# Twenty-seven matrix products whose results nobody reads, taken out of a two-block transformer kernel

## The chip, the cores and the metric

One core of a Trainium2 chip runs the whole kernel. The metric is the device time of one execution in microseconds, lower is better. All arithmetic is in 32-bit floating point.

## What is computed

One sequence of 256 tokens with 1024 features goes through two models, one behind the other.

```python
def reference(x, c, ctx, ...):
    x = first_block(x, c, ctx, ...)
    return second_block(x, c_2, ...)

# first_block, layer 0: short convolution mixer and SwiGLU, on x and on the context
mod = jax.nn.silu(c) @ w_ada[i] + b_ada[i]
mod_c = jax.nn.silu(c_ctx) @ w_ada[i] + b_ada[i]
h = _modulate(_rms_norm(x, norm_mix[i]), sh1, sc1)
hc = _modulate(_rms_norm(ctx, norm_mix[i]), sh1c, sc1c)
# layer 1: neighbourhood attention (x against x and the context) and SwiGLU, on x

# second_block: a norm and one wide projection, sparse attention and an RWKV-7
# recurrence side by side, gated and merged; then a mixture of experts
p_group = jax.nn.softmax((xt @ wg_router).astype(f32), axis=-1)
g_sel = jnp.argmax(p_group, axis=-1)                       # one of 4 groups
top_v, top_i = lax.top_k(e_in, TOP_K_EXPERTS)              # 2 of its 8 experts
acc + cw[:, None] * ((jax.nn.silu(xt @ wg) * (xt @ wu)) @ wd)   # over 32 experts
```

The weights of the 32 experts are 201 MB of the 419 MB that the kernel reads.

## The kernel before, in words

The program is written engine by engine: each engine has its own list of instructions in a fixed order, and semaphores order the lists among each other. No scheduler and no pool moves anything. Activations lie feature-major in SBUF (128 features by 256 tokens for each of 8 slices). SyncE (`block.sync`, line 507) streams all weights into rings of slots in one order, each load behind a wait for the products that last used the slot. GpSimd loads the modulation weights of later layers and adds up halves of weights, VectorE and ScalarE make the norms, the activations and the attention's softmax, and TensorE does the products.

The stages that matter here:

- **Start.** `ada_first(s)` (line 1239) multiplies the two condition vectors by block `s` of four blocks (2 MB each) of modulation weights; each call waits for its block with `slot_landed`. Between the calls stand the first norm's sums (`norm_sums`, line 1259) and the spread of its reciprocal roots over the partitions (`norm_spread`, line 1268). Behind the fourth block ScalarE copies the four rows out (line 856), `ada_columns` turns them into columns (line 1249), VectorE makes shift and scale of them (lines 2329 and 2315), and ScalarE (line 867) and VectorE (line 2730) apply these to the normed activations, slice by slice. The first products of the convolution (lines 1319 and 1327) take the slices as they come.
- **Attention of the second block.** `dsa_attention` on TensorE goes over pairs of heads: scores, a piece of a gate's projection (line 1575) as filling, transposes (line 1598), products with the values.
- **Last norm and router.** `norm(5)` is `norm_sums`, a wait for ScalarE and VectorE, and `norm_spread`. Then come the router's logits (line 2242), their transposes (line 2249), and transposes of the activations (line 2252). VectorE finds the group and the two experts in a chain of 20 small instructions (lines 3119 to 3134). The rank products (lines 2260 to 2264) give each token its place at its experts, VectorE turns them into places and into the count of the busiest expert, and each engine loads this count into a register and branches on it (`count_of`, line 495).
- **Experts.** `pe_gathered` gathers the tokens of four experts with one-hot products (line 1676), goes through gate and up weights (line 1726) and down weights (line 1708), eight times four experts. SyncE has loaded the first four slots of gate and up weights ahead; the load that follows (line 567) waits for the first of TensorE's products to free its buffer, and all further loads follow on it in the same manner.

`keep_on(bank, n)` issues `n` products of the identity with 256 columns of the constants into a PSUM bank that nobody reads. It waits for nothing and signals nothing:

```python
def keep_on(bank, n):

    for i in range(n):
        pe.matmul(PS[:, bank, 0:256], ident, C[:, 0:256], start=True, stop=True)
```

One 32-bit product is two MATMUL instructions and two LDWEIGHTS in the trace.

Of the kernel before, what the change touches and what calls it, by code (L numbers as in the profile page):

```python
# [156 lines left out]
def build(nc, xin, ada, cond, vecs, consts, colmask, dist, reset, rpb, rank_c, W, out):  # L157
    plan = plan_stream()
    MMB = count_products()
    with ExitStack() as ctx:  # L160
# [13 lines left out]
        C = sb("C", NCONST)  # L174
# [10 lines left out]
        PS = ctx.enter_context(nc.psum_tensor("PS", [P, 8, 512], F32))  # L185
# [9 lines left out]
        ident, ones, bo64 = con("ident"), con("ones"), con("bo64")  # L195
# [41 lines left out]
        NORMS = [(0, 0, 2, 0), (24, 0, 2, 0), (0, 1, 2, 0), (24, 1, 1, 0), (0, 2, 1, 1), (24, 2, 1, 1)]  # L237
# [987 lines left out]
        def _(pe):  # L1225
            pe.wait_ge(sem("cond"), 1)
            pe.wait_ge(sem("consts_in"), 16)

            def keep_on(bank, n):

                for i in range(n):
                    pe.matmul(PS[:, bank, 0:256], ident, C[:, 0:256], start=True, stop=True)

            def ada_first(s):

                slot_landed(pe, "ada0", s)
# [34 lines left out]

            def norm(n):
                norm_sums(n)
                keep_on(4, NORMS[n][2] + 1)
                norm_spread(n)
                keep_on(4, 2)

            def norm_ahead(n, left):

# [300 lines left out]
            def dsa_attention():  # L1580
# [33 lines left out]
                for p in range(pairs):  # L1614
                    if p + 1 < pairs:
                        scores(p + 1)
                    gate_part(0, 7, GATE_CUTS[p], GATE_CUTS[p + 1])
                    turn(2 * p)
                    if p == 0:
                        keep_on(5, 3)  # L1620
                    turn(2 * p + 1)
                    if p >= 1:
                        pv(p - 1)
# [233 lines left out]
            norm_sums(0)  # L1857
            ada_first(1)
            norm_spread(0)
            keep_on(4, 4)  # L1860
            ada_first(2)
            keep_on(4, 4)
            ada_first(3)
            ada_columns()
            keep_on(4, 2)
            conv_in_folded()
            conv_out_folded()
            ffn_in_folded()
# [120 lines left out]
            for i in range(12):  # L1989
# [12 lines left out]
                if i == 6:  # L2002
                    for k in range(KD):
                        g = 32 * (k % 4)
                        mm = pe.matmul(PS[g:g + 32, 7, 0:SEQ], vec("w_i", k * 8, k * 8 + 32), XN[:, k * SEQ:(k + 1) * SEQ],
                                       start=(k < 4), stop=(k >= 4))
                    mm.then_inc(sem("wi_mm"), 1)
                if i == 8:
                    pe.wait_ge(sem("wi_done"), 1)
                    for t in range(2):  # L2010
                        mm = pe.matmul(PS[:, 7, 256 + t * 8:264 + t * 8], WIT[:, t * P:(t + 1) * P], con("eight"),
                                       start=True, stop=True)
# [146 lines left out]
            for c in range(NCH):  # L2159
# [3 lines left out]
                for hp in range(HP):  # L2163
                    for h in range(2):
                        dst = PS[64 * h:64 * h + 64, 0, hp * 64:hp * 64 + 64]
                        if c:
                            pe.matmul(dst, f64(KK, c, hp, h), st[64 * h:64 * h + 64, hp * 64:hp * 64 + 64],
                                      start=True, stop=False)
# [21 lines left out]
                for hp in range(HP):  # L2190
                    for h in range(2):
                        dst = PS[64 * h:64 * h + 64, 2, hp * 64:hp * 64 + 64]
                        pe.matmul(dst, c64(BT, c, hp, h), SA[64 * h:64 * h + 64, hp * 64:hp * 64 + 64],
                                  start=True, stop=False)
                        mm = pe.matmul(dst, c64(KT, c, hp, h), c64(VT, c, hp, h), start=False, stop=True)
                mm.then_inc(sem("state_mm"), 1)
                for hp in range(HP):
                    for h in range(2):
                        o = (hp % 2) * 256 + c * CH
                        dst = PS[64 * h:64 * h + 64, 3 + hp // 2, o:o + CH]  # L2200
                        if c:
                            pe.matmul(dst, st[64 * h:64 * h + 64, hp * 64:hp * 64 + 64], f64(RR, c, hp, h),
                                      start=True, stop=False)
# [50 lines left out]
                                      ident)  # L2254
                mm.then_inc(sem("xt_mm"), 1)

            keep_on(4, 7)
            pe.wait_ge(sem("indicated"), 1)
            pe.wait_ge(sem("rank_in"), 16)
            pe.matmul(PS[:, 6, 0:NE], UPPER, IND[:, 0, :], start=True, stop=True)  # L2260
# [1 line left out]
            pe.matmul(PS[:, 6, NE:2 * NE], UPPER, IND[:, 1, :], start=False, stop=True)  # L2262
            pe.matmul(PS[:, 6, 2 * NE:3 * NE], ones, IND[:, 0, :], start=True, stop=False)
            pe.matmul(PS[:, 6, 2 * NE:3 * NE], ones, IND[:, 1, :], start=False, stop=True).then_inc(sem("ranked"), 1)
            keep_on(4, 3)
            busiest = count_of(pe)
            with pe.If(busiest < CAP + 1):
                pe_gathered()
# [1053 lines left out]
```

## Time and profile before

| | us |
|---|---|
| median of 3 runs | 1849.72 |
| lowest and highest | 1849.64, 1849.98 |
| profiled execution, whole | 1848.07 |
| its span, first to last instruction | 1845.9 |
| busy in it: TensorE | 1647.6 |
| VectorE | 920.6 |
| ScalarE | 278.6 |
| GpSimd | 521.1 |

The profile is of one execution. The difference of 2.2 us between its time and its span lies around the program. "PE" is TensorE's products, "PEld" its weight loads, which run beside them; "DVE" is VectorE, "ACT" ScalarE, "POOL" GpSimd, "SP" SyncE. An instruction is named by its line, and what it writes and reads by `out<-in`. "Idle before" is the pause of the engine ahead of an instruction, with the instruction or transfer that ended it; the ends of products are modelled. The granted clock is the share of TensorE's 2.4 GHz that the chip let through: 1.00 is 2.4 GHz and 0.50 is 1.2 GHz. It is recorded where it changes, so that the view shows 1.00 ahead of the first record.

### The profile page before, as it was taken

The page shows a single profiled execution, that of the slowest core. Times are in us where ns is not written, and L with a number is a line of the kernel's source. Part 1 is how long each engine was busy: PE and PEld are TensorE (multiplying, and loading weights), DVE is VectorE, ACT ScalarE, POOL GpSimd, SP SyncE. Part 2 cuts the span into 40 slices and gives each one's busy share as a digit, 9 for nine tenths or more (in the row PEclk, how much of TensorE's full clock was granted, in tenths as well). Part 3 has the DMA queues.
Part 4 walks back from the last instruction along what each step waited for, and adds up shares of the span by engine and source line. Part 5 has one row for each costly group of instructions (what it writes and reads, how often), then busy time and mean ns, then how long its engine had stood idle before and what let it go on. Part 6 is the DMA issues. An engine that isn't in the chain of part 4 may idle for free.

```text
span 1845.9 us, 26016 instructions
## 1 busy us (share of the span) xinstructions
PE 1647.6 (89%) x11170; PEld 1284.0 (70%) x11170; DVE 920.6 (50%) x1439; ACT 278.6 (15%) x612; POOL 521.1 (28%) x375
## 2 busy tenths in 40 slices
PE   6999999999999999999999999999999745574547
PEld 3888778888888868768999887778786312221223
DVE  3999678888672465683876534565223000000001
ACT  3000130000000221272001022341202000000000
POOL 2554455667632249001773212300000000000000
PEclk9999999999999999999999999999999887887779
DMA  9552134557441440025665980520097999999998
GB/s 398 190 228 103 69 142 170 171 180 274 167 156 63 160 183 1 15 85 226 224 228 225 365 327 1 200 81 26 2 399 306 424 430 432 428 432 429 434 431 339
DMA packets 44047, 422.02 MB, mean 229 GB/s; under 512 B 4912, under 2 KB 5312, under 8 KB 22944
## 3 DMA queue, kind: packets, MB, share of 16 engines
q1 hardware_dynamic: 24336, 345.26, 45.9%
q0 software_dynamic: 19168, 72.74, 11.1%
q10 hardware_dynamic: 432, 2.42, 0.4%
q8 instruction: 84, 1.38, 0.3%
q14 instruction: 27, 0.22, 0.0%
HBM read 419.35 MB, written 1.05 MB: 228 GB/s over the span
## 4 chain that ended last, share of the span: by engine, by line
PE 78%; DMA 16%; DVE 3%; issue 1%; ACT 1%; SPq 0%; POOL 0%; ACTq 0%; DVEq 0%; POOLq 0%
DMA ring<-w_gu 15%; PE PS L1425 14%; PE PS L1496 7%; PE PS L1338 7%; PE PS L1469 7%; PE PS L1905 4%; PE PS L1955 4%; PE PS L1543 4%; PE PS L1575 3%; PE PS L1559 3%; PE PS L1726 3%; PE PS L1362 2%; PE PS L1683 2%; PE PS L1676 2%; PE PS L2234 1%
## 5 line engine op out<-in xcount | busy, mean ns | idle before, releaser
L1708 PE MATMUL PS<-A,SC 128*32 128x512 f32 x448 | 62.8, 709 | 126.6 <-DMA A<-w_dn 120.1
L1425 PE MATMUL PS<-ring 128*128 128x256 f32 x672 | 148.5, 379 | 0.0
L1425 PEld LDWEIGHTS PS<-ring 128*128 128x128 f32 x672 | 127.7, 190 | 17.4
L1726 PE MATMUL PS<-ring,SC 128*32 128x512 f32 x768 | 100.4, 680 | 35.9 <-DMA ring<-w_gu 35.9
L1708 PEld LDWEIGHTS PS<-A,SC 128*32 128x32 f32 x448 | 15.5, 122 | 163.3 <-DMA A<-w_dn 126.5
L1425 PE MATMUL PS<-A,ring 128*128 128x256 f32 x504 | 112.2, 379 | 0.0
L2307 DVE CUSTOM_DVE_ANT_0 ring<-ring,SC,V 128x1024 f32<-128x1024 f32 x64 | 106.8, 1691 | 1.3 <-DMA ring<-ada 1.2
L1425 PEld LDWEIGHTS PS<-A,ring 128*128 128x128 f32 x504 | 95.8, 190 | 13.4 <-issue 0.5
L1726 PEld LDWEIGHTS PS<-ring,SC 128*32 128x32 f32 x768 | 25.6, 124 | 108.9 <-issue 66.7
L1338 PE MATMUL PS<-A,ring 128*128 128x256 f32 x456 | 100.2, 379 | 0.0
L2307 DVE CUSTOM_DVE_ANT_0 A<-A,SC,V 128x1024 f32<-128x1024 f32 x64 | 91.7, 1449 | 14.3 <-DMA A<-ada 14.3
L1496 PE MATMUL PS<-A,ring 128*128 128x256 f32 x440 | 95.8, 379 | 0.0
L1338 PEld LDWEIGHTS PS<-A,ring 128*128 128x128 f32 x456 | 86.6, 190 | 12.2 <-issue 0.5
L2645 DVE COPY SC<-PS 128x512 f32<-128x512 f32 x7 | 4.8, 692 | 178.3 <-PE PS L1708 178.3
L1496 PEld LDWEIGHTS PS<-A,ring 128*128 128x128 f32 x440 | 83.6, 190 | 11.4
L1469 PE MATMUL PS<-A,ring 128*128 128x128 f32 x800 | 91.0, 275 | 0.0
L1469 PEld LDWEIGHTS PS<-A,ring 128*128 128x128 f32 x800 | 90.2, 192 | 0.1
L2528 DVE RECIPROCAL SC<-SC 128x256 f32<-128x256 f32 (+1 forms) x24 | 54.8, 2285 | 65.3 <-ACT SC L924 65.2
L619 POOL DMA_DIRECT2D ring<-ada x64 | 34.9, 546 | 173.6 <-ACT A L954 90.9
L1955 PE MATMUL PS<-A,ring 128*128 128x256 f32 x368 | 82.1, 380 | 0.0
L1955 PEld LDWEIGHTS PS<-A,ring 128*128 128x128 f32 x368 | 69.6, 190 | 11.2 <-issue 2.0
L1543 PE MATMUL PS<-A,ring 128*128 128x256 f32 x352 | 76.1, 379 | 0.0
(486 smaller groups left out, 3091.8 us busy)
## 6 DMA issues: line engine op xcount, KB each, us to landing
ring<-w_gu SPq DMA_DIRECT2D x24, 4096.0 KB, 36.0
A<-w_dn SPq DMA_DIRECT2D x31, 2048.0 KB, 31.3
ring<-ada POOLq DMA_DIRECT2D x64, 512.0 KB, 4.6
A<-ada POOLq DMA_DIRECT2D x64, 512.0 KB, 5.5
A<-w_gu SPq DMA_DIRECT2D x7, 4096.0 KB, 35.8
ring<-w_fin SPq DMA_DIRECT2D x22, 1024.0 KB, 6.5
ring<-w_fout SPq DMA_DIRECT2D x16, 1408.0 KB, 8.2
ring<-w_fin SPq DMA_DIRECT2D x11, 2048.0 KB, 8.6
```

Source lines behind the costliest of these rows:

```text
L1338: mm = pe.matmul(PS[:, bank, half * 256:half * 256 + 256], left[:, k], right[:, k], start=(k == 0), stop=(k == 3))
L1425: mm = pe.matmul(PS[:, bank, half * 256:half * 256 + 256], left[:, k], right[:, k], start=(k == 0), stop=(k == 3))
L1469: mm = pe.matmul(PS[:, bank, half * 256 + o:half * 256 + o + P], weights[:, k, o:o + P], tokens[:, k], start=(k == 0), stop=(k == 3))
L1496: mm = pe.matmul(PS[:, bank, half * 256:half * 256 + 256], left[:, k], right[:, k], start=(k == 0), stop=(k == 10))
L1543: mm = pe.matmul(PS[:, FOUT1_BANKS[m % 4], 0:SEQ], slot("fout1", m, k * 128, k * 128 + 128), HID[:, k * SEQ:(k + 1) * SEQ], start=(k == 0) ...
L1559: mm = pe.matmul(PS[:, m % 4, 0:T], slot(stage, m // 4, k * 512 + (m % 4) * 128, k * 512 + (m % 4) * 128 + 128), rhs_of(k), start=(k == 0) ...
L1575: mm = pe.matmul(PS[:, bank, g * 256:g * 256 + 256], slot("gsig", m, g * 1024 + kk * 128, g * 1024 + kk * 128 + 128), XN[:, kk * SEQ:(kk + ...
L1708: mm = pe.matmul(PS[CAP * e:CAP * (e + 1), 2 + half, :], HF[:, q * P + e * CAP:q * P + (e + 1) * CAP], down_slot(n, q, e * D + half * 512, ...
L1726: mm = pe.matmul(PS[CAP * e:CAP * (e + 1), g, :], XG[:, k * P + e * CAP:k * P + (e + 1) * CAP], gate_up_slot(k, w, w + 512), start=(k == 0 ...
L1905: mm = pe.matmul(PS[:, bank, half * 256:half * 256 + 256], left, right, start=(k == 0), stop=(k == 3))
L1955: mm = pe.matmul(PS[:, bank, 0:SEQ], slot("win", i // 4, k * 512 + (i % 4) * 128, k * 512 + (i % 4) * 128 + 128), XN[:, k * SEQ:(k + 1) * ...
L2307: dve.tensor_tensor_reduce(out=JUNK if c == 0 and len(conds) == 2 else ADA[q], in0=ADA[q], in1=CR[:, c * D:(c + 1) * D], scale=1.0, scalar ...
```

## The change

All calls of `keep_on` are taken out, and the function with them: ten products in the start, four around the last norm's spread, three in the attention of the second block, seven ahead of the rank products and three behind them, 27 products or 54 instructions. Nothing is added, and no other instruction changes its place, its operands or its waits; the other engines' lists are the same. (`norm` is called for the last norm alone; `NORMS[5][2]` is 1.)

```diff
--- before.py
+++ after.py
@@ -1226,11 +1226,6 @@
             pe.wait_ge(sem("cond"), 1)
             pe.wait_ge(sem("consts_in"), 16)
 
-            def keep_on(bank, n):
-
-                for i in range(n):
-                    pe.matmul(PS[:, bank, 0:256], ident, C[:, 0:256], start=True, stop=True)
-
             def ada_first(s):
 
                 slot_landed(pe, "ada0", s)
@@ -1271,9 +1266,7 @@
 
             def norm(n):
                 norm_sums(n)
-                keep_on(4, NORMS[n][2] + 1)
                 norm_spread(n)
-                keep_on(4, 2)
 
             def norm_ahead(n, left):
 
@@ -1616,8 +1609,6 @@
                         scores(p + 1)
                     gate_part(0, 7, GATE_CUTS[p], GATE_CUTS[p + 1])
                     turn(2 * p)
-                    if p == 0:
-                        keep_on(5, 3)
                     turn(2 * p + 1)
                     if p >= 1:
                         pv(p - 1)
@@ -1857,12 +1848,9 @@
             norm_sums(0)
             ada_first(1)
             norm_spread(0)
-            keep_on(4, 4)
             ada_first(2)
-            keep_on(4, 4)
             ada_first(3)
             ada_columns()
-            keep_on(4, 2)
             conv_in_folded()
             conv_out_folded()
             ffn_in_folded()
@@ -2254,7 +2242,6 @@
                                       ident)
                 mm.then_inc(sem("xt_mm"), 1)
 
-            keep_on(4, 7)
             pe.wait_ge(sem("indicated"), 1)
             pe.wait_ge(sem("rank_in"), 16)
             pe.matmul(PS[:, 6, 0:NE], UPPER, IND[:, 0, :], start=True, stop=True)
@@ -2262,7 +2249,6 @@
             pe.matmul(PS[:, 6, NE:2 * NE], UPPER, IND[:, 1, :], start=False, stop=True)
             pe.matmul(PS[:, 6, 2 * NE:3 * NE], ones, IND[:, 0, :], start=True, stop=False)
             pe.matmul(PS[:, 6, 2 * NE:3 * NE], ones, IND[:, 1, :], start=False, stop=True).then_inc(sem("ranked"), 1)
-            keep_on(4, 3)
             busiest = count_of(pe)
             with pe.If(busiest < CAP + 1):
                 pe_gathered()
```

Line numbers of the changed kernel are lower by 5 to 14. Two places of TensorE's list, before and now. The first is the start, from the norm's spread to the first product of the convolution (RN holds the reciprocal roots, `ring` the weights, C the constants). Before:

```order
L1268 MATMUL PS<-RN,C 128x128 [waits inverted]
L1268 MATMUL PS<-RN,C 128x128 x3
L1232 MATMUL PS<-C 128x256 x4
L1239 MATMUL PS<-ring,CS 2x512 [waits landed2]
L1239 MATMUL PS<-ring,CS 2x512 x7
L1232 MATMUL PS<-C 128x256 x4
L1239 MATMUL PS<-ring,CS 2x512 [waits landed3]
L1239 MATMUL PS<-ring,CS 2x512 x7
L1249 MATMUL PS<-C,A 128x4x2 [waits rows_copied]
L1249 MATMUL PS<-C,A 128x4x2 x3
L1232 MATMUL PS<-C 128x256 x2
L1319 MATMUL PS<-A,ring 128x256 [waits h_ready,landed4]
```

Now:

```order
L1263 MATMUL PS<-RN,C 128x128 [waits inverted]
L1263 MATMUL PS<-RN,C 128x128 x3
L1234 MATMUL PS<-ring,CS 2x512 [waits landed2]
L1234 MATMUL PS<-ring,CS 2x512 x7
L1234 MATMUL PS<-ring,CS 2x512 [waits landed3]
L1234 MATMUL PS<-ring,CS 2x512 x7
L1244 MATMUL PS<-C,A 128x4x2 [waits rows_copied]
L1244 MATMUL PS<-C,A 128x4x2 x3
L1312 MATMUL PS<-A,ring 128x256 [waits h_ready,landed4]
```

Three rows are gone, and the groups of the third and fourth block follow each other with a wait for each block. The second place is the router, from the transposes of the activations (X) to the gather, with the rank products between (SC holds the router's small tiles). Before:

```order
L2252 MATMUL PS<-C,X 128x128 x12
L1232 MATMUL PS<-C 128x256 x7
L2260 MATMUL PS<-SC 128x32 [waits rank_in,indicated]
L2261 MATMUL PS<-SC,C 128x32
L2262 MATMUL PS<-SC 128x32
L2263 MATMUL PS<-SC,C 128x32
L2264 MATMUL PS<-SC,C 128x32
L1232 MATMUL PS<-C 128x256 x3
L495 TENSOR_LOAD FLAG [waits counted]
L495 ISA x2
L2267 COMPARE_AND_BRANCH
L1676 MATMUL PS<-SC,X 128x128 [waits place,xt_copied]
```

Now:

```order
L2240 MATMUL PS<-C,X 128x128 x12
L2247 MATMUL PS<-SC 128x32 [waits rank_in,indicated]
L2248 MATMUL PS<-SC,C 128x32
L2249 MATMUL PS<-SC 128x32
L2250 MATMUL PS<-SC,C 128x32
L2251 MATMUL PS<-SC,C 128x32
L495 TENSOR_LOAD FLAG [waits counted]
L495 ISA x2
L2253 COMPARE_AND_BRANCH
L1667 MATMUL PS<-SC,X 128x128 [waits place,xt_copied]
```

Two rows are gone: the rank products stand right behind the transposes, and the load of the count right behind the rank products.

## Rows read from the trace of the kernel before

**Rows 1.** The page's 40 slices: granted clock of TensorE in tenths.
```profile
PEclk9999999999999999999999999999999887887779
```

**Rows 2.** Windows: length, busy us (instructions) by engine, clock, DMA share, GB/s.
```profile
36.00:1395.00 1359.00, 1347.21 (x8827) 1149.70 (x8826) 872.10 (x1298) 238.75 (x537) 518.12 (x366) 1.00 0.44 165
1409.33:1412.16 2.83, 2.67 (x16) 2.20 (x17) 1.44 (x11) 0.30 (x2) 0.00 (x0) 1.00 0.00 0
1440.00:1840.00 400.00, 236.13 (x1782) 97.95 (x1778) 21.74 (x49) 18.17 (x36) 0.00 (x0) 0.80 1.00 425
```

**Rows 3.** Timeline of the SyncE queue, 1400 to 1420 us: start, us, instruction.
```profile
1417.88 2.04 SPq L567 DMA_DIRECT2D A<-w_gu  x2
```

**Rows 4.** Timeline of TensorE, the start; last column: idle before, releaser.
```profile
14.43 3.59 PE L1239 MATMUL PS<-ring,CS 128*2 128x512 f32 x16 [14.43 <-DMA ring<-w_ada]
...
23.43 1.89 PE L1232 MATMUL PS<-C 128*128 128x256 f32 x8
25.25 1.90 PE L1239 MATMUL PS<-ring,CS 128*2 128x512 f32 x16
27.08 1.99 PE L1232 MATMUL PS<-C 128*128 128x256 f32 x8
30.06 1.90 PE L1239 MATMUL PS<-ring,CS 128*2 128x512 f32 x16 [0.99 <-DMA ring<-w_ada]
32.73 1.06 PE L1249 MATMUL PS<-C,A 128*128 128x8 f32 x8 [0.78 <-ACT A L856]
...
35.22 7.14 PE L1319 MATMUL PS<-A,ring 128*128 128x256 f32 x32 [0.46 <-ACT A L867]
```

**Rows 5.** Timeline of TensorE, router and gather.
```profile
1399.97 3.64 PE L2242 MATMUL PS<-X,V 128*36 128x256 f32 x16 [0.19 <-ACT X L871]
...
1405.74 3.19 PE L1232 MATMUL PS<-C 128*128 128x256 f32 x14
1409.33 0.41 PE L2260 MATMUL PS<-SC 128*128 128x32 f32 x2 [0.40 <-DVE SC L3134]
...
1410.46 1.54 PE L1232 MATMUL PS<-C 128*128 128x256 f32 x6
1412.16 3.81 PE L1676 MATMUL PS<-SC,X 128*128 128x128 f32 x32 [0.16 <-issue]
```

**Rows 6.** Timeline, attention of the second block.
```profile
1187.16 1.46 PE L1232 MATMUL PS<-C 128*128 128x256 f32 x6
```

**Rows 7.** The chain that ended last, pieces in order of time: start, us, what.
```profile
1396.73 1.06 PE PS L1232 x4
...
1410.63 1.38 PE PS L1232 x6
```

**Rows 8.** Windows in the experts' stage, columns as in rows 2.
```profile
1440.60:1445.90 5.30, 0.01 (x2) 0.00 (x0) 0.00 (x0) 0.00 (x0) 0.00 (x0) 0.76 1.04 445
1445.90:1449.30 3.40, 3.39 (x16) 0.80 (x20) 0.00 (x0) 0.00 (x0) 0.00 (x0) 0.50 1.05 453
1641.50:1644.50 3.00, 3.00 (x16) 0.75 (x20) 0.00 (x0) 0.00 (x0) 0.00 (x0) 0.50 0.99 421
1645.00:1650.00 5.00, 5.00 (x32) 3.23 (x25) 0.69 (x1) 0.60 (x1) 0.00 (x0) 1.00 1.01 429
```

**Rows 9.** Waits of TensorE, 40 to 1400 us: waited for, us, times, longest.
```profile
PE PS L1883 <- DVE A L2530: 1.3, 1, 1.3
```

**Rows 10.** The loads of the modulation weights: issues, and time to landing.
```profile
L507 SPq DMA_DIRECT2D ring<-w_ada x4: 381/433/450, 4.1 to 5.5; - x4
...
DMA to landing us min/median/max: 10.2/16.9/24.5
```

**Rows 11.** First norm's weight loads, before and behind 20 us: ns min/median/max.
```profile
L1259 PEld LDWEIGHTS PS<-A,C x36: 173/173/177, 16.9 to 19.3; 128*32 128x32 f32 x36
...
L1259 PEld LDWEIGHTS PS<-A,C x12: 110/110/110, 20.2 to 20.4; 128*32 128x32 f32 x12
```

## The prediction

> **What bounds the kernel now.** I read the slices of the page first, then the busy time by stretches, then the two places of the change in the timeline, and last what the clock did elsewhere. The slices show TensorE's granted clock near full speed until the experts begin, and lower from there on [rows 1]. The stretches say why [rows 2]: from 36 to 1395 us TensorE is busy for 1347.21 of 1359 us, so every delay of it is a delay of all that follows; from 1440 to 1840 us the DMA engines are busy all the time (share 1.00) and TensorE for 236 of 400 us, so there the expert weights set the pace and a slow TensorE costs nothing. The two meet at one instruction: the load of the expert weights that restarts the stream is issued at 1417.88 [rows 3], behind a stretch in which the DMA share is 0.00 [rows 2], and it waits for the first expert products of TensorE. So the end moves one for one with the time at which TensorE gets to that point. At the very start it is otherwise: the third and fourth groups of the modulation products wait for weights, the fourth until 30.06 [rows 4]; only from there on does TensorE's time count.
>
> **The removed products themselves: 0.** 27 products go, each two instructions. None signals anybody and nobody reads their bank. In the start the eight that stand ahead of 30.06 end before the weights are there; the two behind 32.73 end before 35.22, where the next product waits for a ScalarE result [rows 4]. The seven in the router run from 1405.74 for 3.19 us, and the next product waits for a VectorE result at 1409.33 [rows 5]. The three in the attention (1.46 us from 1187.16) lie in a wait for VectorE too [rows 6]. The last three, from 1410.46 for 1.54 us, end 0.16 us before the gather; but the gather waits for a count that VectorE makes behind the rank products, a load into a register and a branch, which the products do not hold up, so I take 0. The bound on the other side is what the chain of waits has under their name, 1.06 + 1.38 = 2.44 us [rows 7].
>
> **What their absence does to the clock.** They fill pauses. What a pause does is to be seen in the experts: in the 5.30 us pause before 1445.90 the granted clock falls (0.76 on average, and 0.50 behind it), and another fall, before 1641.5, looks the same; TensorE then works at 1.2 GHz for 3.0 to 3.4 us at least, and from 1645 it is at 2.4 GHz again [rows 8]. A pause of 1.3 us amid other work, the longest up to 1395, leaves no mark in the clock [rows 1, 9]. The sixteen instructions at 14.43, the first of the program, take 3.59 us against 1.90 for the same sixteen at 25.25 [rows 4], which is half the pace, so a fall costs half of the time that a busy engine spends at the low level: for 3.0 to about 4.3 us of dense work, 1.5 to 2.1 us.
>
> *Start.* Without the four products at 23.43 and the four at 27.08 TensorE waits for the third block of weights, does its group and waits for the fourth. The third block's landing is an estimate: the fourth is used at 30.06 and the first at 14.43 [rows 4], so blocks come 5.2 us apart, which puts it at 24.9; the median of 16.9 us to landing over issues at 4.1 to 5.5 [rows 10] puts the middle of the second and third landing at 21.7, and the third half a step on, at 24.2. With a group of 1.90 us the engine ends at 26.1 to 26.8 and is idle until 30.06, for 3.3 to 4.0 us. That is nearer to 5.30 than to 1.3: I take it that the clock falls. Then:
> - the fourth group takes 3.59 instead of 1.90: +1.7. It is on the path: the copy of its rows, the columns at 32.73 and the scales follow on it.
> - the four column products (1.06 us) are set by loading weights of 128 columns. Between no loss and a doubling: 0 to +1.1, taken in the middle, +0.5, since no row has such loads at the low level.
> - behind the group come two more pauses, of 0.8 and about 1.4 us (33.79 to 35.22), the second now empty, so either the clock is still low at the first convolution product or falls again there. The products from there are dense: 1.5 to 2.1, and 0 if it has come back by then. I take 1.7, for the two pauses with 1.1 us of work between them.
> Sum +3.9; ends 1.7 and 4.9. Nothing takes it back: the 12 us in which TensorE is idle up to 1395 [rows 2] are waits for results that themselves follow from its products.
>
> *Router.* Without the seven and the three products TensorE has nothing from 1405.9 (the transposes that precede them end there) to 1412.16 but the five rank products at 1409.33, which are done in 1.3 us [rows 5]: 3.4 us of nothing, 1.3 of short products, 1.4 of nothing. I take it that the clock falls in it. Then:
> - the rank products, again set by loads of 128 columns, lose 0 to 1.3. It is open whether the fall comes before them or behind: +0.6.
> - the gather (3.81 us from 1412.16) and the first group of expert products up to the issue at 1417.88 are 5.7 us of dense work. 1.5 if the clock comes back after 3.0, 2.9 if not before the issue: +2.0.
> Sum +2.6; ends 1.5 and 4.2.
>
> *Second norm and attention.* In the last norm 3.2 us lie between 1396.73 and the logits at 1399.97 [rows 5, 7], a third of them the spread, so the pauses around it are about 1.0 and 1.1 us; in the attention one of 1.5 to 1.8 us is left [rows 6]. Both are near the 1.3 that left no mark: 0. If the clock falls there, 1.5 to 1.8 each. So all of it is +3.9 + 2.6 = +6.5. The profiled execution took 1848.07 us (span 1845.9); the terms are differences within it and are added to the median of the runs, 1849.72: 1856.2.
>
> **A rule against these prices.** Of the loads, the rows show this: those of 32 columns take 173 ns at the low level, in the first norm, and 110 ns at the full one [rows 11]; those of 128 columns are shown at the full level only. The Trainium skill, "TensorE: Matmul & The Clock Gate", section "LDWEIGHTS (loading the stationary operand)", gives a load's time by its columns alone, with no word of the clock. By that rule the products that are set by loads would lose nothing; the 32-column rows here speak against it.
>
> **Rivals.**
> - *The loads keep their pace at 1.2 GHz.* The column products, the rank products and the gather (3.81 us for 32 instructions, 119 ns each, a 128-column load each) then lose nothing. Left are +1.7 and +1.7 in the start and, in the router, half of the 1.7 us between the gather's end and the issue, +0.9: +4.3, 1854.0. For it: no row of such loads at the low level. Against it: 173 against 110.
> - *The clock falls in one place only.* Start alone 1853.6, router alone 1852.3. For it: 3.3 us is not 5.3, and the rank products stand in the middle of the router's pause.
> - *It falls in the last norm or the attention as well:* about 1.8 more for each, 1858 to 1860. For it: in the norm two pauses with nothing between them but eight short instructions.
> - *Nothing happens:* the clock holds over these pauses, and the products were in nobody's way: 1849.7. This is also what a change that takes out only idle filling would do. For it: the page's slices show the full level all the way to 1400; but that is with the products in.
> - *Faster.* The last three products hold up the queue of TensorE ahead of the gather, and two ahead of the spread of the last norm: the chain of waits passes through them for 2.44 us [rows 7]. If that is real waiting, it goes: 1847.3. It decides if the clock does not fall, and the products before the gather start within 0.16 us of their predecessor because of it and not of the branch. Against it: the next steps wait for VectorE's results, which come at the same time as before.
>
> **How the numbers follow.** Forecast (both falls) 0.60, loads keep their pace 0.12, one place only 0.10, further places 0.08, nothing 0.07, faster 0.03. The forecast's own ends are 3.2 and 9.1. For the range I take 1851.5 to 1860.0: it leaves out nothing, faster, and about a twentieth above. A measurement of this kernel tells 0.2%, 3.7 us, from no change, so slower begins at 1853.4. The forecast's range (1852.9 to 1858.8) lies above it but for its lowest end, the first rival by a little, of "one place" the start. Slower 0.80, within 0.2% 0.18, faster 0.02 (even that rival is within).
>
> **What would show it.** In the profile of the changed kernel: the fourth modulation group at some 3.6 us instead of 1.90, the convolution's first product 1.7 to 2.7 us later, and the first 16 instructions of it in more than their share of 7.14 us; a granted clock under 1.00 somewhere between 26 and 42 us and between 1408 and 1418 us; the load of the experts issued 6 to 7 us later than 1417.88, and the same distance from there to the end as before. The prediction is wrong if the clock reads 1.00 in both places, if the delay at 36 us is not found again at 1395, or if the distance from the load's issue to the end changes.

## The result, and the profile after

The changed kernel takes **1853.89 us** at the median of 16 runs, the kernel before, on the same chip, 1849.37 (16 runs, 1846.93 to 1851.82): 4.5 us more. One of the 16 executions took 5951.64 us, and one of the kernel before in a later set 2514.65; both stand apart and are left out of all that follows. The other 15 of the changed kernel (1852.06 to 1856.38) have their median at 1853.77; the ratio is 1.0028, with a 95% interval of 1.0021 to 1.0034. Forecast were 1856.2 us, +6.5, in a range of 1851.5 to 1860.0. So the direction is right and the time lies in the range, but 2.0 of the 6.5 us are missing, and by the trace not because every term was a little too large: a loss and two gifts that the prediction did not have stand in the result.

The profiled execution of the changed kernel took 1853.23 us (before: 1848.07), its span is 5.3 us longer. The page's slices, to be held against [rows 1]: the first slice has lost its full clock, and the one around 1411 us.

```profile
span 1851.2 us, 25908 instructions
...
PEclk8999999999999999999999999999998877877879
```

The timeline of TensorE in the start (columns as in [rows 4]; line numbers are lower by 5 to 14, as said under the change):

```profile
25.31 3.59 PE L1234 MATMUL PS<-ring,CS 128*2 128x512 f32 x16 [2.91 <-DMA ring<-w_ada]
30.09 3.60 PE L1234 MATMUL PS<-ring,CS 128*2 128x512 f32 x16 [1.19 <-DMA ring<-w_ada]
34.46 1.88 PE L1244 MATMUL PS<-C,A 128*128 128x8 f32 x8 [0.78 <-ACT A L856]
37.76 8.96 PE L1312 MATMUL PS<-A,ring 128*128 128x256 f32 x32 [1.42 <-ACT A L867]
46.56 7.03 PE L1320 MATMUL PS<-A,ring 128*128 128x512 f32 x16
```

The third and the fourth group of modulation products each take 3.6 us instead of 1.90, the column products 1.88 instead of 1.06, the first 32 MATMULs of the convolution 8.96 instead of 7.14. The group behind them began at 42.20 before and begins at 46.56: **+4.4 us**. The windows of the same stretch, of a part of the attention, of the last norm and of the router (columns as in [rows 2]; the granted clock is the last number but two):

```profile
24.50:41.40 16.90, 12.70 (x49) 5.51 (x50) 8.27 (x22) 4.96 (x10) 5.72 (x8) 0.50 1.00 417
1190.00:1193.00 3.00, 1.55 (x7) 0.88 (x5) 2.96 (x3) 0.01 (x1) 2.86 (x2) 1.00 1.02 426
...
36.00:1395.00 1359.00, 1345.80 (x8813) 1148.52 (x8814) 873.81 (x1306) 239.97 (x538) 514.99 (x366) 1.00 0.44 164
...
1403.50:1406.70 3.20, 3.20 (x9) 1.44 (x9) 1.23 (x4) 1.82 (x5) 0.00 (x0) 0.50 1.02 440
1413.70:1420.40 6.70, 5.17 (x24) 5.07 (x25) 2.49 (x14) 0.28 (x2) 0.00 (x0) 0.50 0.01 2
```

The clock is at 0.50, that is 1.2 GHz, in the start, in the row of logits behind the last norm and in the router, and at 2.4 GHz in the attention although its pause is there. The timeline from the last norm on, which answers to [rows 5]:

```profile
1397.93 1.42 PE L1254 MATMUL PS<-SC,C 128*32 128x64 f32 x64
1400.37 1.10 PE L1263 MATMUL PS<-RN,C 128*128 128x64 f32 x8 [1.02 <-DVE RN L2322]
1402.58 5.33 PE L2230 MATMUL PS<-X,V 128*36 128x256 f32 x16 [1.11 <-ACT X L871]
...
1413.62 0.63 PE L2247 MATMUL PS<-SC 128*128 128x32 f32 x2 [3.41 <-DVE SC L3120]
...
1417.48 5.22 PE L1667 MATMUL PS<-SC,X 128*128 128x128 f32 x32 [1.53 <-DVE SC L2604]
1422.63 2.78 PE L1717 MATMUL PS<-A,SC 128*32 128x512 f32 x24
```

And the load that restarts the stream of the experts, 6.7 us after its time in [rows 3]:

```profile
1424.62 2.04 SPq L567 DMA_DIRECT2D A<-w_gu  x2
```

**Where the time went.** I matched every product of the two traces and took the difference of their starts. This delay is 4.4 us at 50 us and stays so until 1235 us. Then it *shrinks*, by 1.0 us between 1235 and 1243 us and by 0.8 between 1285 and 1295, and is 2.6 us at 1395. The logits of the norm add 1.7 (4.3), the rank products 1.0 (5.3), the gather and the first expert group 1.4 (6.7). The stream of the experts and the tail give back 1.4 (span +5.3): 0.6 up to 1700 us, 0.9 in the last group of expert products, which takes 5.46 us here and 6.32 in the first trace of the kernel before, but 5.54 in its second. So there is one term that the prediction had put at 0 (the norm), and one gift that it had excluded (at 1238 and 1288 us). What stood there in the kernel before (timeline of TensorE):

```profile
1237.22 0.52 PE L2107 MATMUL PS<-A 64*64 64x64 f32 x12
1238.33 7.60 PE L2107 MATMUL PS<-A 64*64 64x64 f32 x244 [0.59 <-issue]
...
1288.24 0.28 PE L2139 MATMUL PS<-X,A 64*64 64x64 f32 x2 [0.75 <-issue]
```

Two pauses that no semaphore ended, within long rows of small products. They are 1.3 of the 1.8 us; the rest lies in the same rows, without a pause in the trace. The changed kernel passes through the same rows without a pause:

```profile
1235.94 5.81 PE L2079 MATMUL PS<-C,A 64*64 64x64 f32 x192
1241.59 4.60 PE L2095 MATMUL PS<-A 64*64 64x64 f32 x150
```

### The profile page after: what moved, and what is told of

Same layout as the page of the kernel before. It is cut to its first block, busy times and chain, and to the rows that moved or that the text cites. A ratio compares the mean times of both kernels' runs of the same rounds, so it can differ in the third digit from the quotient of the medians.

```text
span 1851.2 us, 25908 instructions
## 1 busy us (share of the span) xinstructions
PE 1642.5 (89%) x11116; PEld 1278.8 (69%) x11116; DVE 920.3 (50%) x1439; ACT 278.7 (15%) x612; POOL 517.9 (28%) x375
## 3 DMA queue, kind: packets, MB, share of 16 engines
q8 instruction: 84, 1.38, 0.3%
## 4 chain that ended last, share of the span: by engine, by line
PE 78%; DMA 16%; DVE 3%; issue 1%; ACT 1%; SPq 0%; POOL 0%; ACTq 0%; DVEq 0%; POOLq 0%
DMA ring<-w_gu 15%; PE PS L1418 14%; PE PS L1331 7%; PE PS L1489 7%; PE PS L1462 7%; PE PS L1893 4%; PE PS L1943 4%; PE PS L1536 4%; PE PS L1568 3%; PE PS L1552 3%; PE PS L1717 3%; PE PS L1355 2%; PE PS L1667 2%; PE PS L1674 2%; PE PS L2222 1%
```

## The experiments

Theory: each group of products holds the clock up in its own place, and its absence costs half of the time that TensorE then works at 1.2 GHz. Rivals: the cost is not the clock but the changed list of instructions; or one place carries it all. Every kernel below computes the full result; the products taken out, shortened or added are read by nobody. Times are medians, with the number of runs. The experiments ran in three sets, each with runs of the kernel before beside it: 1848.66 us (27 runs), 1848.39 (34) and 1849.19 (32). A difference, as +1.2, is always to the kernel before of the same set, and kernels of different sets are compared by these differences. Delays in a trace are against the first trace of the kernel before.

### One place at a time

**The start's ten products out.**

```diff
-            keep_on(4, 4)
             ada_first(2)
-            keep_on(4, 4)
             ada_first(3)
             ada_columns()
-            keep_on(4, 2)
```

> Only the ten products of the start are left out. Clock theory: the third group of modulation products ends and TensorE waits about 3 us, the clock is at 0.50 somewhere between 24 and 42 us, the first convolution product comes 2.5 us later than in the kernel before (35.22) and the blocks behind it 4.3 us later; the kernel is 3.5 to 4.5 us slower, if nothing gives it back before the experts. Rival, the delay is given back: the products from 50 us on are 4 us late, at 1395 us 2.6 or less, and the kernel is 0 to 2.6 us slower. In the last norm and the router the clock stays at 1.00.

1849.88 us (11 runs), ratio 1.0005 (0.9996 to 1.0014): +1.2, not told from nothing by the times, though its trace shows a loss of 3.2 us in the start. So the rival of the expectation came. The clock falls at 29.83 and again at 36.66, the delay is 3.2 us from 50 to 1235 us; then it drops by 0.8 and by 0.9, as in the changed kernel, and is 1.4 at 1395. The two rows of small products have no pause here either:

```profile
1235.79 4.77 PE L2088 MATMUL PS<-C,A 64*64 64x64 f32 x157
1240.39 5.78 PE L2104 MATMUL PS<-A 64*64 64x64 f32 x184
```

**The last norm's four out.**

```diff
                 norm_sums(n)
-                keep_on(4, NORMS[n][2] + 1)
                 norm_spread(n)
-                keep_on(4, 2)
```

> Only the four products around the last norm's spread are left out. Clock theory as the changed kernel's profile shows it: the clock falls in the logits in some executions and not in others, 0 to 1.7 us for an execution, 0.5 to 1.7 in the median. The prediction on record took 0 here. Rival: the fall in the changed kernel came from its position in time alone and the median is the same within 0.3 us.

1850.41 us (11), ratio 1.0009 (1.0000 to 1.0019): +1.8, at the edge of what the times tell. The trace shows the fall, as long a logits row as in the changed kernel, and pauses of the same 1.02 and 1.11 us:

```profile
1398.79 1.10 PE L1268 MATMUL PS<-RN,C 128*128 128x64 f32 x8 [1.02 <-DVE RN L2334]
1401.01 5.29 PE L2240 MATMUL PS<-X,V 128*36 128x256 f32 x16 [1.11 <-ACT X L871]
```

The delay grows by 1.65 us there, so these four were not idle filling. The same trace holds a surprise: the clock also falls at 35.62 in the start, *with* its ten products in place, which costs 1.7 us.

**The router's ten out** (`keep_on(4, 7)` and `keep_on(4, 3)`).

> Only the seven and three products of the router are left out. Clock theory: the clock falls between 1406 and 1413 us, the rank products take up to twice their 1.3 us, the gather up to 7 instead of 3.8, the load of the experts is issued 1.5 to 4.2 us later than in the kernel before, 2.5 as in the changed kernel, and the kernel is as much slower. Rival, the products stood in the queue: 0 to 1.4 us faster.

1850.56 us (11), ratio 1.0012 (1.0003 to 1.0021): +1.9. In its trace the fall comes among the rank products (at 1409.66) instead of at the first one, the gather takes 5.75 us, and the delay grows by 0.5 and then by 1.9 up to 1418 us:

```profile
1409.06 0.41 PE L2259 MATMUL PS<-SC 128*128 128x32 f32 x2 [3.42 <-DVE SC L3132]
...
1412.42 5.75 PE L1676 MATMUL PS<-SC,X 128*128 128x128 f32 x32 [1.53 <-DVE SC L2616]
```

**The attention's three out** (`keep_on(5, 3)`).

> Only the three products of the attention are left out. Prediction on record: 0, the pause of 1.65 us lets the clock be. Clock rival: the clock falls there in some executions, up to 1.8 us slower. Code-place theory: the pauses near 1238 and 1288 us change by the 12 instructions, 0 to 1.4 us faster.

1849.55 us (10), ratio 1.0006 (0.9997 to 1.0015): +1.2, not told from nothing by the times. Its trace shows a pause of 1.61 us, and the clock at 0.50 behind it, which costs 1.6 us (windows of this kernel in the second fence):

```profile
1188.37 0.33 PE L1598 MATMUL PS<-C,A 128*128 128x128 f32 x1 [0.15 <-DVE A L2549]
1190.31 0.33 PE L1598 MATMUL PS<-C,A 128*128 128x128 f32 x1 [1.61 <-DVE A L2549]
```

```profile
1192.00:1195.00 3.00, 3.00 (x13) 2.16 (x11) 1.39 (x8) 1.10 (x6) 0.00 (x0) 0.50 1.01 423
```

The changed kernel has that pause too (1.62 us) and kept its clock. Of the four traces with this pause three fell; what decides it was not found.

### Clock or list

**All 27 products kept, of 8 columns instead of 256.**

```diff
-                    pe.matmul(PS[:, bank, 0:256], ident, C[:, 0:256], start=True, stop=True)
+                    pe.matmul(PS[:, bank, 0:8], ident, C[:, 0:8], start=True, stop=True)
```

> All 54 instructions stay where they are, but each product has 8 columns instead of 256, so the engine's list has the same length and the engine next to no work in them. Clock theory: as the changed kernel, 3.5 to 5.5 us slower than the kernel before, with the clock at 0.50 in the start and in the router. Rival, it is the length of the list (where code is fetched, where the queue stands): as the kernel before, within 0.5 us, clock 1.00 in both places.

1856.35 us (5), ratio 1.0041 (1.0027 to 1.0055): +7.7. The list is as long as that of the kernel before, each instruction in its place, and yet the clock falls in the start, behind the norm and in the router. This settles the slowdown for the clock. It is +7.7 where the changed kernel is +4.5, but the intervals overlap and these are five runs, so the times do not tell the two apart. The trace has the pauses at 1238 and 1288 us as before (0.59 and 0.75 us), so the gift is missing: the delay shrinks by 0.2 us up to 1395 and not by 1.8. But the start costs less in this execution (1.6 us), the norm 1.5 and the router 3.6, so the trace does not show how the difference of the medians comes about.

```profile
1401.31 5.17 PE L2242 MATMUL PS<-X,V 128*36 128x256 f32 x16 [0.71 <-ACT X L871]
...
1412.18 0.64 PE L2260 MATMUL PS<-SC 128*128 128x32 f32 x2 [1.95 <-DVE SC L3134]
...
1414.34 1.43 PE L1232 MATMUL PS<-C 128*128 128x8 f32 x6
1416.06 6.40 PE L1676 MATMUL PS<-SC,X 128*128 128x128 f32 x32 [0.30 <-issue]
```

### What gives time back at 1238 and 1288 us

New theory: these pauses hang on how many instructions stand ahead of them. **Sixteen more instructions of products, 8 columns wide, ahead of the fourth modulation group of the kernel before** (and as many weight loads):

```diff
             keep_on(4, 4)
+            for i in range(8):
+                pe.matmul(PS[:, 4, 0:8], ident, C[:, 0:8], start=True, stop=True)
             ada_first(3)
```

> The kernel before with eight products of 8 columns more (32 instructions) in the wait for the fourth block of weights, about 1 us of short work where 0.99 us is idle. Nothing else changes, so the clock is as before. Code-place theory: the two pauses of TensorE that no semaphore ends, 0.59 us ahead of the transposes' products near 1238 us and 0.75 near 1288 us in the kernel before, are of another length or gone, since all code behind the start lies 32 instructions further; the time moves by up to 1.4 us to either side. Rival, the pauses went in the changed kernel because it is late: both pauses are here as before, within 0.1 us.

1847.86 us (10), ratio 0.9992 (0.9983 to 1.0002): −0.5, which the times do not tell from nothing. The trace shows more: one pause has moved into an earlier row of products and grown to 1.30 us, the one at 1288 us is gone.

```profile
1235.78 2.38 PE L2093 MATMUL PS<-C,A 64*64 64x64 f32 x76
1239.46 0.33 PE L2093 MATMUL PS<-C,A 64*64 64x64 f32 x4 [1.30 <-issue]
```

**The start's ten products out, ten of 8 columns put in at one place**, so that the list from 35 us on has its old length and the clock falls all the same. This is the run that decides about the gift:

```diff
-            keep_on(4, 4)
             ada_first(2)
-            keep_on(4, 4)
             ada_first(3)
             ada_columns()
-            keep_on(4, 2)
+            for i in range(10):
+                pe.matmul(PS[:, 4, 0:8], ident, C[:, 0:8], start=True, stop=True)
```

> The start's ten 256-column products are out as in the run without them, but ten products of 8 columns stand behind the column products, so that TensorE's instruction list has its old length from 35 us on, while the clock should fall in the start as before. Theory that the give-back (1.6 us at 1238 and 1288 us) comes from the shorter list ahead of two pauses without a releaser: the delay at 50 us is 3 to 4 us as without the padding, the pauses of 0.6 and 0.5 to 0.75 us are back, and the delay at 1395 us is still 3 to 4 us; median 1.3 to 3 us above the run without padding, so about 1851 to 1852.5. Rival, that the pauses vanish because TensorE runs later: they stay away, the delay at 1395 us is 1.5 us and the median about 1849.9.

1853.07 us (11), ratio 1.0025 (1.0016 to 1.0034): +3.9, where the kernel without the padding is +1.2; the intervals do not overlap. Both pauses are back, larger than before (1.18 and 0.83 us), and the delay does not shrink between 1235 and 1395 us but grows, from 5.7 to 6.1:

```profile
1242.91 0.52 PE L2106 MATMUL PS<-A 64*64 64x64 f32 x12
1244.61 1.61 PE L2106 MATMUL PS<-A 64*64 64x64 f32 x47 [1.18 <-issue]
...
1294.36 0.28 PE L2138 MATMUL PS<-X,A 64*64 64x64 f32 x2 [0.83 <-issue]
```

That the pauses vanished only because TensorE ran later is thereby refuted: it runs 5.7 us late here, 4.4 in the changed kernel, and they are back. Between the two traces the stretch from 1235 to 1395 us makes 2.2 us of difference and the start's clock, 5.7 us here and 3.2 there, another 2.5, together more than the 2.7 us between the medians. How the medians divide is not shown.

**What the pauses are.** The page has a queue for instructions (q8, 84 pieces, 1.38 MB, so 16 KB each). It is TensorE's: up to 1400 us, 255 to 256 instructions of TensorE (products and weight loads) lie on average between the starts of two pieces, in each of the 14 traces. The transfers in narrow windows, of the kernel before, of the padded one and of the changed one:

```profile
q8 instruction: 1, 0.02, 4.9%
```

```profile
q8 instruction: 1, 0.02, 5.2%
```

```profile
q8 instruction: 1, 0.02, 4.8%
```

The windows are 1235.8 to 1237.0, 1242.1 to 1243.2 and 1240.2 to 1241.4 us; each holds one piece of instructions, starting at 1235.9, 1242.2 and 1240.3. In the first two kernels the pause ends 2.4 us after that start, at 1238.33 and 1244.61. With the longer list the piece starts at 1237.1 and the pause ends at 1239.46, again 2.4. At the second place it is 1286.0 and 1288.24, and 1292.0 and 1294.36 with the padding. In the 14 traces of this case TensorE has 20 pauses of over 0.2 us at these two places, none of them with a releaser, and every one ends 2.1 to 2.45 us after the start of a piece. The reading that fits is that TensorE runs out of instructions here, where a MATMUL takes 0.03 us, and waits for the next piece; where the boundary of a piece falls behind other products, the same fetch costs nothing. The shifts of the list bear this out: gone with the start's ten products out, back with the padding, moved by 32 instructions more. It stays an inference; why the piece is asked for no earlier is open.

Two limits. The pauses also differ where the list ahead of them is the same: the run with the norm's four out, which stand behind both places, has 0.33 and 0.55 us, and in the five traces (that one among them) whose list up to there is as long as before, the delay shrinks by 0.2 to 0.7 us from 1235 to 1395. So of the 1.8 us some 0.4 are the first trace's own, and the shorter list gives back about 1.4. And not every pause without a releaser is of this kind: one of 0.32 us near 673 us stands in all 14 traces, 6 to 28 us behind the last piece, whatever the list.

### The same kernels once more

**The kernel before** and **the changed kernel**, unchanged, for a second trace of each.

> The kernel before, once more, as a second profile and a null comparison. Ratio 1.000 within 0.0008. Theory that part of its spread comes from the start: either the first group of weights and the norm show the same clock as in the first profile, or a fall of about 1.7 us behind 34 us as in two of the variants that kept these products; the pauses at 1238 and 1288 us stay at 0.6 and 0.5 to 0.75 us either way.

> The changed kernel, once more: 4 to 5 us above the kernel before. Theory: falls in the start, in the last norm and in the router again, the pauses at 1238 and 1288 us gone again; the attention's pause of about 1.6 us may fall or not (it did not in the first profile, it did with its products alone out), and with a fall the delay grows by 1.6 us there. If the two pauses were chance rather than the list's length, they come back here.

Before: 1848.14 us (11), ratio 0.9997 (0.9988 to 1.0006). Against the first trace it is never off by more than 0.3 us from 27 to 1418 us. Changed: 1854.71 us (10), ratio 1.0027 (1.0017 to 1.0036), so the result repeats. But the profiled execution, 1856.69 us and the slowest of its ten, lost its time elsewhere: 1.9 us in the start (2.5 less than the first), 1.7 in the attention, nothing in the norm although its pauses are 1.02 and 1.11 us as before, 3.9 in the router, and 4.0 at 1080 us. The gift came again, 1.0 and 1.1 us. The loss at 1080 us is not the change's: the trace of the tail experiment below, which has all products in, shows it too. There a block of `ada` lands late, 14.3 us after its issue (14.5 in the second trace of the changed kernel, 7.7 and 7.9 in the first traces of the two kernels). The timeline of VectorE, then of TensorE, in the tail experiment:

```profile
1077.82 1.28 DVE L2310 CUSTOM_DVE_ANT_0 A<-A,SC,V 128x1024 f32<-128x1024 f32 x1 [3.74 <-DMA A<-ada]
```

```profile
1080.01 0.32 PE L1259 MATMUL PS<-A,C 128*32 128x64 f32 x8 [2.27 <-ACT A L846]
```

TensorE waits 2.27 us for it and goes on at the low clock.

### Can both be beaten?

The kernel before waits 5.06 us for the last block of expert weights and then does the last 32 MATMULs with that block, 3.6 us of work, in 6.32 us. **Ten products of 256 columns in that wait:**

```diff
+                        if last and k == 6:
+                            pe.wait_ge(sem("ys_act"), it)
+                            keep_on(2, 10)
                         if k % 2 == 0:
                             gate_up_landed(pe, trip, n, k // 2)
```

> The kernel before with ten products more in the last group of experts, in the 5 us wait for the last quarter of its gate and up weights. In the kernel before the clock falls in that wait and the 32 instructions behind it take 6.32 us instead of about 3.6; the last down weights are loaded only behind them. Theory, that this end is the one place in the experts where the clock counts: 1.5 to 2.7 us faster, and a smaller spread from run to run. Rival, the end waits for transfers anyway: the same within 0.5 us.

1848.02 us (11), ratio 0.9999 (0.9990 to 1.0008). The 32 MATMULs do take 3.64 us, and the trace has gained 2.7 us behind them; 1.2 of these are lost again before the end, where TensorE now waits 0.94 us for down weights. No gain can be told from the times. **With it, the start's products as five of 512 columns and two of 256, and the attention's out:**

```diff
-            keep_on(4, 4)
+            keep_wide(2)
             ada_first(2)
-            keep_on(4, 4)
+            keep_wide(2)
             ada_first(3)
+            keep_on(4, 1)
             ada_columns()
-            keep_on(4, 2)
+            keep_wide(1)
+            keep_on(4, 1)
...
-                    if p == 0:
-                        keep_on(5, 3)
```

> The kernel before with three edits: the start's ten products as five of 512 columns and two of 256, one of them in the wait ahead of the column products, so that no pause is left in which the clock fell in one profile (1.7 us); no products in the attention; ten products in the last group's wait. Each theory by itself gives 0 to 1.7 us (start), 0 to 1.4 us (code 24 instructions shorter ahead of 1238 us) and 1.5 to 2.7 us (end): 2 to 4.5 us faster than the kernel before.

1847.52 us (12), ratio 0.9996 (0.9988 to 1.0005): inconclusive. `keep_wide(n)` is n products of 512 columns. In its trace the clock fell in the attention again (1.6 us) and not in the start, and it fell in the tail in spite of the ten products, behind a wait of 2.02 us that they left open:

```profile
1817.92 5.34 PE L1732 MATMUL PS<-ring,SC 128*32 128x512 f32 x32 [2.02 <-DMA ring<-w_gu]
```

**The same with the attention's products kept:**

> The kernel before with fewer but 512-column products in the waits of the start (same columns and more, 14 instructions less), the three attention products kept, and ten products before the last w_dn loads are waited for. Theory: no fall in start, norm, attention and router, the pauses without a releaser shrink by up to 1.6 us as in the run without the start's products, the tail keeps its clock: 1 to 3 us less than the kernel before, 1846 to 1847.5. Rival, that the pauses only move with the list and the tail is then set by the weights' landing: 1848 to 1849, no difference.

**1845.92 us** (11), ratio 0.9982 (0.9973 to 0.9991): 3.3 us less than the kernel before, 8.8 less than the changed one in the same set. The tail of the kernel before, and then of this one (timelines of TensorE):

```profile
1816.77 6.32 PE L1726 MATMUL PS<-ring,SC 128*32 128x512 f32 x32 [5.06 <-DMA ring<-w_gu]
```

```profile
1810.37 4.58 PE L1232 MATMUL PS<-C 128*128 128x256 f32 x20
1816.07 3.64 PE L1734 MATMUL PS<-ring,SC 128*32 128x512 f32 x32 [1.11 <-DMA ring<-w_gu]
```

In its trace the tail gives 2.7 us (delay −0.7 at 1816, −3.4 at 1824), or 1.9 against the second trace of the kernel before, whose 32 MATMULs took 5.54 us. The two pauses are 0.35 and 0.48 us instead of 0.59 and 0.75, which one trace with the old list has too (0.33 and 0.55). How the 3.3 us divide was not tried: the wide products stood in no run alone, and the tail alone showed no gain in the times.

## Why the prediction was right and wrong

**What bounds the kernel: right.** The delay of the start is carried to 1235 us without loss, and the load that restarts the stream is issued 6.74 us later for an end 5.3 us later. From there to the end of the span it was 428.0 us and is 426.6; in the second traces 426.9 and 427.4, and 426.5 to 428.5 over the eleven traces whose tail was left alone. So "one for one" holds within 1 to 2 us. The prediction's sign that this distance must not change is missed by 1.4 us, which is within what executions of one kernel differ by; the clock in the last group of expert products makes 0.9 of it.

**The removed products cost nothing themselves: right.** The 2.44 us of chain [rows 7] were no real waiting. Behind the seven in the router, TensorE now waits 3.41 us for the same VectorE result. The "faster" rival falls with that.

**The start, +3.9: measured +4.4, right in mechanism, by another course.** The fourth group +1.7 as forecast. The column products +0.8, in the range of 0 to 1.1. The convolution +1.8 where 1.7 was taken. What I had not seen is that the clock falls before the third group: that group, at half pace, takes 1.7 us out of the long pause that I had computed (3.3 to 4.0 us; what is left is 2.91 before the third group and 1.19 before the fourth), and hides its own loss in the wait for the weights. How much the start costs varies more than my ends said: 4.4, 1.9, 3.2 and 5.7 us in four traces without its products, and with the products as before, the clock still fell there in two of seven, which cost 1.5 and 1.7 us.

**The router, +2.6: measured +2.4**, rank products +1.0 (of 0 to 1.3; 0.6 taken), gather and first group +1.4 (2.0 taken); +2.5 in the trace with the router's products alone out, and +3.9 in the second trace, near the upper end of 4.2.

**The loads do lose their pace.** The rival that left them out (1854.0) comes near in time and is wrong in mechanism. The rank products come 0.43 us apart at 1.2 GHz, 0.23 before. The weight loads of the gather, before and after, in ns of one (the number behind the comma):

```profile
L1676 PEld LDWEIGHTS PS<-SC,X 128*128 128x128 f32 x32 | 3.6, 192 | 0.5 <-issue 0.5
```

```profile
L1667 PEld LDWEIGHTS PS<-SC,X 128*128 128x128 f32 x29 | 4.7, 259 | 1.6 <-issue 1.6
...
L2250 PEld LDWEIGHTS PS<-SC,C 128*128 128x128 f32 x2 | 0.5, 333 | 0.0
```

The gather's 259 mixes both levels; the rank products' 333 is the low one alone, against 192. The rule of the Trainium skill ("TensorE: Matmul & The Clock Gate", "LDWEIGHTS (loading the stationary operand)"), by columns alone, does not hold here: the same 128 columns take 192 or 333 ns as the clock is. Nor do the times go with the columns at one level: at 2.4 GHz 32 columns take 110 ns [rows 11], more than half of 192.

**The last norm, 0: wrong, +1.7.** I had put its pauses (1.0 and 1.1 us, measured 1.02 and 1.11) beside the wait of 1.3 us that left no mark [rows 9] and weighed each by itself. But that one stands amid dense work, and these two stand around eight short MATMULs. The run with them alone out shows +1.65 in the trace and +1.8 in the times. The rival "it falls in the last norm or the attention as well" (0.08) had this right, at the price that it gave: 1.5 to 1.8 where it falls. The attention's 0 is half wrong: with the same pause of 1.61 us it kept its clock in one trace of the changed kernel and lost 1.6 to 1.7 us in three other traces.

**"Nothing takes it back": wrong, −1.8.** This is the step that failed in the argument. That the time came out as near as it did is luck: the norm's +1.7, taken as 0, and this −1.8 cancel, and neither was forecast. I had looked at the 12 us of idle time up to 1395 [rows 2] and called them waits for results. 1.3 us of them had no releaser at all (the two rows of before above). By the reading above they were waits for instructions, and taking out 13 products, 52 instructions with their weight loads, moved the boundaries of the pieces by a fifth of a piece. The start's products, alone out, show 1.2 us in the times, where their trace shows 3.2 of loss and 1.7 given back. My own test in the prediction, that the delay at 36 us must be found again at 1395, passes by its letter, and by luck: the convolution's first product is 2.54 us late, and 2.61 are left at 1395. What it was to show, that all of the start's delay is carried to the experts, failed: 4.4 from 46 us on, 2.6 at 1395.

**The sum.** In the first trace: 4.4 − 1.8 + 1.7 + 2.4 − 1.4 at the end = 5.3, the difference of the spans. In the times the four places alone give 1.2 + 1.8 + 1.9 + 1.2 = 6.1 against 4.5 for all; with intervals of about 1.7 us either way on each, that is no contradiction, nor is it proof that they add up.

## What to carry to other kernels

Products that nobody reads are not ballast until the granted clock behind each pause has been looked at, and a pause of 1 us beside another one can matter as much as one of 3; one trace does not tell, since the same pause falls or holds from one execution to the next. A change in the number of instructions can move pauses without a releaser in a stretch of short instructions: look at such pauses, and at the starts of the instruction queue's pieces, before calling a difference of 1 or 2 us the effect of an edit, and give a control the same number of instructions. Where a wait is filled to hold the clock, fewer and wider products can do it with a shorter list: the clock held in the start in both traces with products of 512 columns, as in five of the seven with 256; that the width matters is not shown.

## What the runs showed of the hardware that I had not expected

- TensorE's clock fell behind pauses of 1.02 and 1.11 us around 1.1 us of work in two of three traces, and behind one of 1.61 us in three of four. One of 1.3 us amid dense work was followed by no fall in any of the 14 traces.
- TensorE paused for 0.25 to 1.3 us with no releaser, each time until 2.1 to 2.45 us after a 16 KB piece of its instructions began to move (20 pauses); read here as a wait for its own instructions.
- Weight loads of 128 columns take 192 ns at 2.4 GHz and 333 at 1.2; the rank products, which go with such loads, go from 0.23 to 0.43 us apart.
- One transfer of `ada` near 1080 us landed late in 2 of 14 traces and cost 3.8 to 4.0 us, 2.3 to 2.4 of waiting and the rest of clock. It is one source of the 5 to 7 us by which executions of one kernel differ within a set.
